# Two transformer blocks on one core: the low parts of the MLPs' weights made by an adding DMA in place of a GpSimd subtraction

## The reference

```python
def sq_relu_mlp(u, w_up, w_down):            # first block, D_FF = 4 * D_MODEL = 4096
    hdn = jax.nn.relu(u @ w_up)
    return (hdn * hdn) @ w_down
...
h = h + sq_relu_mlp(rms_norm(h, norm2_g), w_up, w_down)
...
h2 = rmsnorm(x, g_norm2) * (1.0 + scale2) + shift2
x = x + gate2 * (jnp.square(jax.nn.relu(h2 @ w_mlp1)) @ w_mlp2)
```

## Time and profile before

| | |
|---|---|
| median of the two runs | 1353.1 us (1353.09 and 1353.11) |
| span of the profiled execution | 1351.4 us, 1.7 us under the median of the runs |
| TensorE matmuls busy | 1340.5 us, 99% |
| VectorE, ScalarE, GpSimd busy | 754.1, 526.0, 563.0 us (56%, 39%, 42%) |
| granted clock | full in nearly every slice |
| DMA queue of SyncE and ScalarE | 154.43 MB, 39.5% of the 16 engines' span |

### The profile page before, as it was taken

How to read it: one execution, slowest core, us unless ns; L and a number is a source line. 1 busy time by engine, 2 the same in 40 slices (tenths; PEclk the granted TensorE clock), 3 DMA queues, 4 the chain that set the end, 5 groups by cost and what they waited for, 6 DMA issues and landing times.

```text
span 1351.4 us, 18070 instructions
## 1 busy us (share of the span) xinstructions
PE 1340.5 (99%) x6380; PEld 1093.9 (81%) x6380; DVE 754.1 (56%) x1085; ACT 526.0 (39%) x830; POOL 563.0 (42%) x230
## 2 busy tenths in 40 slices
PE   9999999999999999999999999999999999999998
PEld 8888878888888888876877777888878888888886
DVE  3555578475664654878788774444463241432355
ACT  6344234322323324254366655322355133142333
POOL 5334334453553635524222223444434534345351
PEclk9999999999999999999999999999999999999999
DMA  7232245555665655423222323333423423324231
GB/s 230 79 93 83 90 124 167 167 172 174 197 175 163 176 150 163 112 92 96 62 63 79 95 64 94 109 94 109 125 71 102 125 76 111 93 79 123 78 94 63
DMA packets 212807, 155.74 MB, mean 115 GB/s; under 512 B 8932, under 2 KB 193760, under 8 KB 212744
## 3 DMA queue, kind: packets, MB, share of 16 engines
q1 hardware_dynamic: 212280, 154.43, 39.5%
q10 hardware_dynamic: 464, 0.48, 0.1%
HBM read 152.75 MB, written 4.74 MB: 117 GB/s over the span
## 4 chain that ended last, share of the span: by engine, by line
PE 53%; DVE 1%; ACT 1%; issue 0%; POOL 0%; ACTq 0%; DVEq 0%
PE ps L580 28%; PE ps L1126 11%; PE ps L1070 3%; PE ps L1007 2%; PE ps L986 1%; PE ps L973 1%; PE ps L1156 1%; PE ps L959 1%; PE ps L960 1%; PE ps L963 0%; PE ps L946 0%; PE ps L920 0%; PE ps L921 0%; PE ps L924 0%; DVE nt L2267 0%
## 5 line engine op out<-in xcount | busy, mean ns | idle before, releaser
L541 POOL TENSOR_TENSOR w_lo<-raw,w_hi 128x1024 fp32r<-128x1024 f32 x222 | 560.0, 2530 | 758.2 <-ACT w_hi L1212 738.1
L580 PE MATMUL ps<-u_hi,w_hi 128*128 128x512 f32 x944 | 378.3, 401 | 0.7 <-POOL w_lo L541 0.5
L580 PE MATMUL ps<-u_hi,w_lo 128*128 128x512 f32 x944 | 368.4, 390 | 0.0
L580 PE MATMUL ps<-u_lo,w_hi 128*128 128x512 f32 x944 | 367.8, 390 | 0.0
L1212 ACT ACTIVATE w_hi<-raw 128x1024 fp32r<-128x1024 f32 x222 | 231.6, 1053 | 290.7 <-PE ps L580 112.5
L580 PEld LDWEIGHTS ps<-u_hi,w_lo 128*128 128x128 f32 x944 | 177.2, 188 | 37.7
L580 PEld LDWEIGHTS ps<-u_hi,w_hi 128*128 128x128 f32 x944 | 178.2, 189 | 36.1 <-issue 1.6
L580 PEld LDWEIGHTS ps<-u_lo,w_hi 128*128 128x128 f32 x944 | 177.6, 188 | 35.2 <-issue 1.0
L580 PE MATMUL ps<-y_hi,w_hi 128*128 128x512 f32 x320 | 125.2, 391 | 0.1
L580 PE MATMUL ps<-y_hi,w_lo 128*128 128x512 f32 x320 | 124.5, 389 | 0.0
L580 PE MATMUL ps<-y_lo,w_hi 128*128 128x512 f32 x320 | 124.5, 389 | 0.0
(11 more groups left out here) (317 smaller groups left out, 1878.4 us busy)
## 6 DMA issues: line engine op xcount, KB each, us to landing
raw<-w_in SPq DMA_DIRECT2D x69, 512.0 KB, 3.8
raw<-w_mlp SPq DMA_DIRECT2D x64, 512.0 KB, 4.0
adaw<-w_ada SPq DMA_DIRECT2D x32, 768.0 KB, 4.5
raw<-w_up SPq DMA_DIRECT2D x32, 512.0 KB, 6.6
raw<-w_down SPq DMA_DIRECT2D x32, 512.0 KB, 6.0
raw<-w_out SPq DMA_DIRECT2D x16, 512.0 KB, 4.4
bias_rows<-bias_rows SPq DMA_DIRECT2D x4, 635.0 KB
xtok<-x SPq DMA_DIRECT2D x4, 512.0 KB, 7.5
```

What stands on the lines that cost most here:

```text
L541: pool.tensor_tensor(w_lo[:, s, :], raw[:, s, :], w_hi[:, s, :], ALU.subtract).then_inc(lo_ready[s], 1)
L580: last = pe.matmul(ps[0:cols, bank, :], w[:, s, c], r[:, k, :], start=(k == ks[0] and w is w_hi and r is r_hi), stop=(k == ks[-1] and w is ...
```

## The change

Only the two MLPs change (`summed=True`). ScalarE, after it has rounded `raw` into `w_hi`, also writes its negative into `w_lo`. GpSimd no longer subtracts: it issues a DMA that adds `raw` onto `w_lo` in SBUF, 512 KB, and goes on. TensorE and SyncE wait for the landing of that DMA, on semaphores of its own (`lo_summed`, 16 for each landing), where they waited for the subtraction. 64 low parts of each MLP are made so; the other 94 are subtracted as before.

`hi_ready` counts two for each turn in the MLPs, so `Stage` holds the counts of the three semaphores apart. GpSimd's loops over these two stages and ScalarE's loop at the second output projection are unrolled. Three other semaphores are merged into neighbours to make room (`bfor_in` into `rope_in`, `conv_y3` into `conv_taps`, `fgate_z` and `mean_sq` into `fgate_log` and `factor`).

```diff
     def landed(self, s, i):
         return self.raws[s] + 16 * self.dmas[s] * (i + 1)
+    def low(self, s, i):
+        return self.sums[s] + 16 * i if self.summed else self.lows[s] + i
+    def high(self, s, i):
+        return self.highs[s] + self.high_step * i
...
-    st_mlp = Stage(st_out, NF * 4, 4)
+    st_mlp = Stage(st_out, NF * 4, 4, summed=True)
...
-    st_mlp2 = Stage(st_out2, NF * 4, 4)
+    st_mlp2 = Stage(st_out2, NF * 4, 4, summed=True)
...
+        def low_made(st, s):
+            return (lo_summed if st.summed else lo_ready)[s]
...
                 sp.wait_ge(raw_ready[s], st.raws[s])
-                wait(sp, lo_ready[s], st.turn(s, i))
+                wait(sp, low_made(st, s), st.low(s, i))
+                if st.summed:
+                    sp.wait_ge(lo_ready[s], st.lows[s])
+                elif st.sums[s]:
+                    sp.wait_ge(lo_summed[s], st.sums[s])
...
             def lo(st, s, i):
-                pool.wait_ge(hi_ready[s], st.turn(s, i) + 1)
-                pool.tensor_tensor(w_lo[:, s, :], raw[:, s, :], w_hi[:, s, :], ALU.subtract
-                                   ).then_inc(lo_ready[s], 1)
+                pool.wait_ge(hi_ready[s], st.high(s, i + 1))
+                if st.summed:
+                    pool.dma_start(w_lo[:, s, :].bitcast(F32), raw[:, s, :], accum_op=ALU.add).then_inc(lo_summed[s], 16)
+                else:
+                    pool.tensor_tensor(w_lo[:, s, :], raw[:, s, :], w_hi[:, s, :], ALU.subtract
+                                       ).then_inc(lo_ready[s], 1)
...
                 if opens:
-                    pe.wait_ge(lo_ready[s], st.turn(s, i) + 1)
+                    pe.wait_ge(low_made(st, s), st.low(s, i + 1))
                     wait(pe, bank_free[s], st.turn(s, i))
...
                 act.activation(w_hi[:, s, :], raw[:, s, :], ACT.Copy).then_inc(hi_ready[s], 1)
+                if st.summed:
+                    act.wait_ge(hi_ready[s], st.high(s, i) + 1)
+                    act.activation(w_lo[:, s, :], w_hi[:, s, :], ACT.Copy, scale=-1.0).then_inc(hi_ready[s], 1)
+
+            follows = {st_out: st_mlp, st_mlp: st_idx, st_out2: st_mlp2}
 
             def ahead(st, s, i):
                 t = s + AHEAD
                 if t >= st.k:
                     t, i = t - st.k, i + 1
+                if isinstance(i, int) and i == st.n and st in follows:
+                    st, i = follows[st], 0
                 cast(st, t, i)
...
-            with act.Fori(0, KC // 4) as i:
+            for i in range(KC // 4):
                 for s in range(4):
                     ahead(st_out2, s, i)
```

More of the change, by code:

```diff
@@ L151, with __init__ @@
 class Stage:
-    def __init__(self, before, n, k, dmas=()):
+    def __init__(self, before, n, k, dmas=(), summed=False):
         self.base = [b + (before.n if before and s < before.k else 0)
@@ L159, in __init__ @@
                      for s, b in enumerate(before.raws if before else [0] * SLOTS)]
-        self.n, self.k = n, k
+        self.lows = [b + (before.n if before and s < before.k and not before.summed else 0)
+                     for s, b in enumerate(before.lows if before else [1] * SLOTS)]
+        self.sums = [b + (16 * before.n if before and s < before.k and before.summed else 0)
+                     for s, b in enumerate(before.sums if before else [0] * SLOTS)]
+        self.highs = [b + (before.high_step * before.n if before and s < before.k else 0)
+                      for s, b in enumerate(before.highs if before else [1] * SLOTS)]
+        self.n, self.k, self.summed = n, k, summed
+        self.high_step = 2 if summed else 1
         self.dmas = list(dmas) or [1] * SLOTS
@@ L553, in _ @@
                         lo(st_bra, s, m)
+                elif st.summed:
+                    for i in range(st.n):
+                        for s in range(st.k):
+                            lo(st, s, i)
                 elif st.n == 1:
@@ L752, in _ @@
             for k in range(1, KC - 2):
-                pe.wait_ge(lo_ready[k // 2], st_rv.turn(k // 2, 0) + 1)
+                pe.wait_ge(lo_ready[k // 2], st_rv.low(k // 2, 1))
                 pe.wait_ge(sem("norm_u"), before("n1") + k + 1)
@@ L760, in _ @@
                     turn_chunks(k + 1)
-            pe.wait_ge(lo_ready[SLOTS - 1], st_rv.turn(SLOTS - 1, 0) + 1)
+            pe.wait_ge(lo_ready[SLOTS - 1], st_rv.low(SLOTS - 1, 1))
             pe.wait_ge(sem("norm_u"), before("n1") + KC)
@@ L887, in idx_units @@
                         if k == 0:
-                            pe.wait_ge(lo_ready[s], st.turn(s, 0) + 1)
+                            pe.wait_ge(lo_ready[s], st.low(s, 1))
                             wait(pe, bank_free[s], st.turn(s, 0))
@@ L904, in idx_units @@
                     pe.matmul(ps[:, OU, :], w_hi[:, 2, k * P:(k + 1) * P], u_lo[:, k, :], start=False, stop=False)
-                pe.wait_ge(lo_ready[2], st.turn(2, 0) + 1)
+                pe.wait_ge(lo_ready[2], st.low(2, 1))
                 for k in range(KC):
@@ L996, in value_slot @@
             def value_slot(r, s, between=None):
-                pe.wait_ge(lo_ready[s], st_val.turn(s, r) + 1)
+                pe.wait_ge(lo_ready[s], st_val.low(s, r + 1))
                 if s == 0:
@@ L1062, in branch @@
             def branch(m):
-                pe.wait_ge(lo_ready[2], st_bra.turn(2, m) + 1)
+                pe.wait_ge(lo_ready[2], st_bra.low(2, m + 1))
                 wait(pe, bank_free[2], st_bra.turn(2, m) - 1)
@@ L1119, in down_rows @@
                 for s in range(SLOTS):
-                    pe.wait_ge(lo_ready[s], st_mlp2.turn(s, n) + 1)
+                    pe.wait_ge(low_made(st_mlp2, s), st_mlp2.low(s, n + 1))
                     def block(kk, i):
@@ L1160, in last_down_rows @@
                 for k in range(KC // 2):
-                    pe.wait_ge(lo_ready[k // 2], st_mlp2.turn(k // 2, n) + 1)
+                    pe.wait_ge(low_made(st_mlp2, k // 2), st_mlp2.low(k // 2, n + 1))
                     for i in range(NT):
```

41 lines of the change are left out of this document (21 added, 20 removed).

## The result

The changed kernel takes **1400.5 us** in the median of two runs (1399.9 and 1401.1), against 1353.1 before: a ratio of 1.0343 with a 95% interval of 1.0311 to 1.0375, slower. The forecast was 1386 with a range of 1353 to 1480. The profiled execution took 1399.9 us with a span of 1397.8, 46.4 us more than the span before.

The account below looks back on a forecast made before the run. The prediction took TensorE, busy 1340.5 of 1351.4 us, as the bound. It added 27 (first MLP's DMA throughput), 3 (its latency) and 3 (second MLP's start), +33, to 1353.1 for 1386 us, range 1353 to 1480.

Parts of the forecast that it names:

- The bound and what costs nothing: Whole kernel: TensorE bounds it, so GpSimd's 320 us less, the merged semaphores and the unrolled loop are worth 0.
- ScalarE's 135 us of copies: Both MLPs: 128 negating copies of 1.05 us each fit ScalarE's room; the later relu is hidden, each lead shrinks 1.05 us.
- The price of an add, 2.6 us: DMA engines: one 512 KB add costs as much as two plain transfers, 2.6 us, with bounds of 1.3 and 3.5.
- Rival 2: Both MLPs: the adder is slower than a copy, beyond 3.7 us per add; about 1455 to 1650 us; chance 0.21.
- Throughput of the first MLP, +27: First MLP: DMA work of 5.86 us per unit exceeds the 5.44 available by 0.42, over 64 units +27 us.
- The first rival (all hidden): First MLP: the DMA traffic fits, at most 2.2 us per add, so not slower, 1356 us; chance 0.33.
- Latency in the first MLP's up turns, +3: First MLP: adds land after 6.9 to 7.5 us, slot 2 late by up to 0.7 and slot 0 by 0.1; +3 us.
- The start of the second MLP, +3: Second MLP's start: slot 2, rounded late behind the norm, makes TensorE wait 3 us once.
- The granted clock falls: Sign, with TensorE waiting for the relus as the other, that the forecast is wrong altogether; no size given.
- No other wait in the second MLP: Second MLP: adds land after 4.0 to 4.9 us, inside leads of 6.8 and 7.4, so no wait.
- rivals 2 or 3: Rival 3, both MLPs: latency alone, GpSimd's issue taking microseconds, about 1450 us spread evenly; chance 0.08. Sign: second MLP over 10 us longer.
- SyncE's queue: Raw loads: tiles come free 3.5 to 6 us later behind SyncE's in-order issues; effect counted inside the +27.

Follow-up runs that it names:

- experiment 11: Changed kernel with ScalarE negating and GpSimd subtracting in the second MLP alone, no adding DMA, first MLP as before the change: 1353.7 us, ratio 1.0004.
- experiment 5: Changed kernel with ScalarE's negating copies kept in both MLPs but GpSimd subtracting as before, no adding DMA: 1358.0 us, ratio 1.0033.
- 3: Changed kernel with GpSimd's DMA copying raw onto w_lo without adding, all sizes and waits kept: 1368.8 us, ratio 1.0107.
- 7: Changed kernel with adding DMAs for slots 1 and 3 only in both MLPs, subtractions for slots 0 and 2: 1369.8 us, ratio 1.0120.
- 9: Changed kernel with each w_ada load but the first two cut to an eighth of its columns, all adds kept: 1378.8 us, ratio 1.0191.
- experiment 6: Changed kernel with slot 2 of the second MLP's first turn rounded and negated early, during the norm: 1394.3 us, ratio 1.0310.
- experiment 8: Changed kernel with the fourth bias-row spreading DMA moved to the attention's start, behind its first two table loads: 1392.3 us, ratio 1.0285.
- experiment 10: Changed kernel with slot 2 of the second MLP's first turn made early and the fourth bias-row spread moved to the attention: 1386.5 us, ratio 1.0244.
- 12: Changed kernel with adding DMAs in the second MLP only and slot 2 of its first turn made early: 1359.0 us, ratio 1.0042.

## Why the prediction was right, and where it was not

**The bound and what costs nothing.** Right. GpSimd's relief gave nothing back: every kernel with adds takes longer than the one before. The merged semaphores and ScalarE's unrolled loop cost nothing (experiment 11). ScalarE's 135 us of copies cost 1.0 us at the second MLP's start (5 and 11). In experiment 5 another 3.1 us are lost behind the first MLP; they are open, and the changed kernel doesn't have them.

**The price of an add, 2.6 us.** Right: 2.8 us by the queue's share, 8 packets of 0.327 us, 2.6, by the packets. The rule of the Trainium skill that the forecast set beside its bounds ("Collectives: The Full Stack", section on the bandwidth ceiling: two reads, half the speed) fits the price: 2.8 us is twice the copy's 1.43. That the adding itself is free, as the same section has it, no run here shows. Rival 2 needed more than 3.7 us per add and is out.

**Throughput of the first MLP, +27.** Right in its mechanism: share 0.97, 22.4 us outside the spread's turn. Between 440 and 560 us TensorE has 496 matmuls where it had 534, which is 0.93 of the pace: a unit of 5.44 / 0.93 = 5.86 us, the forecast's number. Over all turns but the spread's, 22.4 us in 60 units make 5.81. That the numbers agree is in part luck, for the sum behind them was rough. The 3.26 us were a share of time, and this share is more than the packets need when nothing holds them up: in the kernel before a 512-byte packet of the weights takes 27 ns in the median and 30 in the mean, a 6144-byte packet of w_ada 234 and 324. By the medians a unit asks for 1024 x 27 / 16 + 64 x 234 / 16 = 2.7 us, and with the add 5.3: just inside 5.44. What was lost is then the price of traffic that comes in bursts on engines with no slack, and experiments 3, 7 and 9 show that this price begins below a share of 1 (0.80 in 7, 0.89 in 9). The first rival (all hidden) fell all the same. The ceiling in the Trainium skill ("DMA: Bandwidth & Descriptors", section Specifications), 435 GB/s, is near what long packets reach here (4096 bytes in 160 ns on 16 engines: 410 GB/s); the weights' packets of 512 bytes reach 303, and the first MLP moved 241 GB/s when its engines were 0.97 busy (an add counts its 512 KB once there, though it costs two copies).

**Latency in the first MLP's up turns, +3.** Not to be told apart from the throughput: adds land after 8.2 us, not 6.9 to 7.5, with the engines full. An estimate from the medians: a load of 8.0 to 8.7 us, the rounding and the negation of 1.05 each and an add of 8.2 make 18 to 19 us of a turn of 21.8, where the forecast had counted 11 for the second MLP and made no such sum for the first.

**The start of the second MLP, +3.** Right in place and mechanism (a wait of 3.7), too small by half: the turn lost 5.8, because the clock fell in this wait and the next dozen matmuls ran at half pace, a term that the forecast did not have. "The granted clock falls" was named as a sign against the whole forecast. It fell, but in the changed kernel only in waits that the adds had caused (and in the last microseconds, as before); in experiment 6, with the wait gone, the low clock at that place is gone.

**No other wait in the second MLP.** This step failed. The forecast gave an add 4.9 us to land and a lead of 6.8; the median was 6.3 and the longest 9.7, since adds meet the loads of `raw` and each other, and 6.2 us were lost in later turns. With plain copies (3) or half as many adds (7) nearly all of this goes: 0.0 and 1.2 us outside the first turn. The second MLP grew by 12.0, over the 10 that was to speak for rivals 2 or 3; with a share of 0.80 it was neither, but a weak form of rival 3 by contention.

**The step that was missed: SyncE's queue.** The forecast counted raw tiles coming free later, but did not look at what else stands in the same queue. A DMA that was harmless when it held back one load for 6.5 us cost 12.0 us, the dearest single place, a quarter of the loss.

Together: 22.4 + 12.0 + 5.8 + 6.2, less 0.2 between the MLPs, is 46.2 of the span's 46.4; the forecast had 27 + 3 (first MLP), 3 and 0. It was 13 us short, but not by one step alone: 12.0 of the DMA, 2.8 of the start and 6.2 of the later turns were missing, 21 us, and the 30 for the rest of the first MLP were 7.6 too many. That these errors partly cancel is luck.

## What to carry to other kernels

An adding DMA cost the engines two copies here, and its place in the budget is the DMA share of the stage where it runs: where the sum nears 1, TensorE pays, and some of it already at 0.8. Before giving a stage more traffic, list every DMA in the queue that feeds the critical slot, not only the regular ones, because the rare large one is what the lost lead exposes. Price a wait of TensorE of several microseconds with the slow matmuls behind it.

## What the runs showed of the hardware

- GpSimd is busy 861 ns with the issue of an adding DMA and 529 ns with a plain one of the same shape:

```profile
L566 POOL DMA_DIRECT2D w_lo<-raw x128 | 67.8, 529 | 640.8 <-ACT w_lo L1246 633.1
```

- At its quickest an add of 512 KB in SBUF landed 4.5 us after its issue, a copy 2.8.
- VectorE's operation on w_ada went from 2946 to 1815 ns when GpSimd no longer worked on tiles beside it, worth nothing here. It is 1815 in experiments 3 and 9 too, which have no subtraction in that MLP either, and 2196 and 3031 in 5 and 7, which have 64 and 32:

```profile
L2037 DVE SCALAR_TENSOR_TENSOR acc<-adaw,vec,acc 128x1536 f32<-128x1536 f32 x28 | 50.8, 1815 | 6.6 <-DMA adaw<-w_ada 4.7 <-DVE y_lo L2091 1.5
```

- The granted clock went to 0.50 in waits of 3.7 and 9.3 us, and stayed there for 6.8 and 10.2 us, well into the work that followed. It is not the same each time: behind the same wait of 3.7 us it was at 0.50 for 3.4 us in experiments 8 and 9. Behind three waits of 1.8 to 2.6 us experiment 10 had dips of 3.4 us, and behind two of 1.9 and 2.6 us experiment 8 had none. Short dips also came at the start of the indexer, behind small matmuls (3.4 us in 9, 10 and 12, 6.8 in 3 and 5); what calls them up is open. The slower executions of one kernel have the lower mean clock: of the kernel before, 1352.4 us at 1.000 and 1355.8 at 0.997.
